# An RWKV scan in chunks: the state kept as one block-diagonal tile for two heads, and a chunk's products grouped by their shape on the array

## The reference, cut to what matters

```python
def step(state, inp):
    r_t, w_t, k_t, v_t, kk_t, b_t = inp
    sa = jnp.einsum('bhij,bhj->bhi', state, -kk_t)
    state = (state * w_t[:, :, None, :]
             + sa[..., None] * b_t[:, :, None, :]
             + v_t[..., None] * k_t[:, :, None, :])
    y_t = jnp.einsum('bhij,bhj->bhi', state, r_t)
    return state, y_t
```

## Time and profile before

| | us |
|---|---|
| median of 3 runs | 1783.13 |
| lowest and highest run | 1780.41, 1783.81 |
| span of the profiled execution | 1782.2 |
| TensorE busy in it (matmuls) | 1641.4 |
| VectorE, ScalarE, GpSimd busy | 882.9, 659.2, 122.8 |

### The profile page before, as it was taken

One profiled execution on the slowest core, in us unless ns is written; L12 is line 12 of the kernel. 1 busy time (PEld: TensorE's weight loads), 2 busy tenths in 40 slices (PEclk: granted clock), 3 DMA queues, 4 the chain that ended last, 5 costly groups with the idle time before them and its releaser, 6 DMA issues.

```text
span 1782.2 us, 36627 instructions
## 1 busy us (share of the span) xinstructions
PE 1641.4 (92%) x15044; PEld 1028.8 (58%) x15044; DVE 882.9 (50%) x1880; ACT 659.2 (37%) x1316; POOL 122.8 (7%) x311
## 2 busy tenths in 40 slices
PE   5999999999899989999999999999999988777798
PEld 2465565654654575868676767676754544333443
DVE  1371450732614466777777777878630542111163
ACT  2151431622412465565646565556510112111113
POOL 7000010000000000000000000000000012121100
PEclk9999999999999999999999999999999979999999
DMA  9230110301200321121202021111044579999831
GB/s 354 90 93 2 47 49 0 96 0 47 95 7 14 99 68 54 31 82 33 71 26 71 28 70 44 53 50 48 3 160 173 212 274 419 421 421 408 319 155 48
DMA packets 105463, 210.95 MB, mean 118 GB/s; under 512 B 10195, under 2 KB 78136, under 8 KB 92029
## 3 DMA queue, kind: packets, MB, share of 16 engines
q1 hardware_dynamic: 99256, 197.52, 30.6%
q0 software_dynamic: 4896, 8.40, 1.3%
q10 hardware_dynamic: 1188, 3.28, 0.5%
HBM read 203.80 MB, written 14.81 MB: 123 GB/s over the span
## 4 chain that ended last, share of the span: by engine, by line
PE 52%; DMA 10%; DVE 4%; ACT 2%; issue 2%; SPq 0%; DVEq 0%; ACTq 0%; POOL 0%; POOLq 0%
PE ps L1452 11%; DMA W<-in_moe_w_up_dram 7%; PE ps L2491 5%; PE ps L1463 5%; PE ps L1624 4%; PE ps L1593 4%; PE ps L3073 3%; PE ps L2887 3%; DMA W<-in_moe_w_gate_dram 3%; PE ps L506 2%; PE ps L1493 2%; PE ps L1474 1%; PE ps L1503 1%; PE ps L1515 1%; PE ps L1478 1%
## 5 line engine op out<-in xcount | busy, mean ns | idle before, releaser
L1452 PE MATMUL ps<-hT,W 128*128 128x512 f32 x512 | 231.8, 597 | 2.2 <-ACTq L95 2.2
L1452 PEld LDWEIGHTS ps<-hT,W 128*128 128x128 f32 x512 | 95.6, 191 | 99.9 <-issue 98.1
L594 PE MATMUL ps<-hT,W 128*128 128x512 f32 x288 | 141.0, 612 | 4.2 <-DVE spare L189 4.2
L1463 PE MATMUL ps<-W,hT 128*128 128x256 f32 x512 | 124.0, 388 | 0.0
L2035 DVE SCALAR_TENSOR_TENSOR arena<-ps,arena 128x510 f32<-128x510 f32 (+1 forms) x128 | 95.4, 745 | 12.3 <-ACT arena L1754 8.9
L1463 PEld LDWEIGHTS ps<-W,hT 128*128 128x128 f32 x512 | 93.1, 190 | 12.8
L2491 PE MATMUL ps<-W,yT 128*128 128x512 f32 x216 | 93.1, 592 | 0.9 <-ACT yT L1847 0.9
L1857 ACT ACTIVATE W<-ps 128x512 f32<-128x512 f32 x96 | 57.5, 599 | 70.9 <-PE ps L1593 30.7
L1624 PE MATMUL ps<-W 64*64 64x64 f32 x2304 | 77.2, 220 | 0.0
L594 PEld LDWEIGHTS ps<-hT,W 128*128 128x128 f32 x288 | 49.4, 190 | 45.9 <-issue 44.2
L2887 PE MATMUL ps<-W,yT 128*32 128x256 f32 x1024 | 59.6, 388 | 17.0 <-DMA W<-in_moe_w_gate_dram 10.7
(11 more groups left out here) (535 smaller groups left out, 2925.7 us busy)
## 6 DMA issues: line engine op xcount, KB each, us to landing
W<-in_w_in_dram SPq DMA_DIRECT2D x33, 512.0 KB, 6.6
W<-in_gdn_w_in_dram SPq DMA_DIRECT2D x16, 1024.0 KB, 7.6
arena<-in_moe_w_up_dram SPq DMA_DIRECT2D x16, 1024.0 KB, 18.4
arena<-in_moe_w_down_dram SPq DMA_DIRECT2D x16, 1024.0 KB, 17.0
W<-in_moe_w_up_dram SPq DMA_DIRECT2D x16, 1024.0 KB, 5.8
W<-in_moe_w_down_dram SPq DMA_DIRECT2D x16, 1024.0 KB, 18.3
W<-in_moe_w_gate_dram SPq DMA_DIRECT2D x16, 1024.0 KB, 17.4
arena<-in_moe_w_gate_dram SPq DMA_DIRECT2D x14, 1024.0 KB, 19.4
```

Of the source, the lines that this page charges most:

```text
L594: mm = pe.matmul(ps[:, 5 + i % 2, :], w[:, k, j, :], hT[:, k, :], start=(k == 0), stop=(k == ND - 1))
L1452: mm = pe.matmul(ps[:, 6 + k0 % 2, :], wg[:, k, j * P:(j + 1) * P], hT[:, k, :], start=(k == 0), stop=(k == ND - 1))
L1463: mm = pe.matmul(ps[:, 4 if t < 2 else 1, 256 * (t % 2):256 * (t % 2) + 256], hT[:, k, t * P:(t + 1) * P], wz[:, k, :], start=(k == 0), st ...
```

## The change

A tile `Sd` of 128x128 is added, `state_diagonal`. Head 0's state stands in its upper left quarter, head 1's in the lower right one, and the other two quarters are set to zero once, by GpSimd, before the loops.

- RU: for `c` above 0, one product of `AR` (all 128 partitions) by `Sd` gives both heads' state part in 128 columns of bank 0, and the two products of `Q` add to the two halves of it. In chunk 0, where the state is zero, only the two products of `Q` are issued.
- Y: its state part is one product, `Sd` by `AR`, issued right behind RU and ahead of slot 0; in chunk 0 it is left out. The other four products of Y add to it. They now stand right behind S1, ahead of slot 2.
- S1 and Y take the two heads in turn for each kind of product, where before they took all kinds for one head and then for the other. In the last chunk S1 is left out, since nothing reads it.
- ScalarE's copy of RU reads one bank.
- VectorE no longer clears `S0` and no longer waits for Y before the scaling. In chunk 0 it scales straight from PSUM. After the scaling it copies the two quarters into `Sd`, and the step that TensorE waits for is counted behind the second copy.

```diff
@@ setup @@
+    Sd = sb("state_diagonal", [P, P])
...
@@ tensor engine, chunk loop @@
-                pe.wait_ge(*rw_dve.at(f"S0 {c}", n))
+                if c:
+                    pe.wait_ge(*rw_dve.at(f"S0 {c}", n))
+                    pe.matmul(ps[:, 0, 0:P], AR[:, c, 0, :], Sd[:], start=True, stop=True)
                 for h in range(2):
                     r = slice(h * HD, h * HD + HD)
-                    pe.matmul(ps[:, 4 * h, 0:HD], AR[r, c, 0, :], S0[r, :], start=True, stop=False)
-                    mm = pe.matmul(ps[:, 4 * h, 0:HD], Q[:, h, c, 2, :], tok[:, c, 2, r], start=False, stop=True)
+                    mm = pe.matmul(ps[:, 0, r], Q[:, h, c, 2, :], tok[:, c, 2, r], start=(c == 0), stop=True, skip_group_check=bool(c))
                 mm.then_inc(*rw_pe.step(f"RU {c}"))
+                if c:
+                    pe.matmul(ps[:, 7, cs], Sd[:], AR[:, c, 1, :], start=True, stop=True)
...
+                if c < NT - 1:
+                    for h in range(2):
+                        r = HALF[h]
+                        pe.matmul(ps[r, 2, 0:HD], tok[:, c, 0, r], U[:, r], start=True, stop=False)
+                    for h in range(2):
+                        r = HALF[h]
+                        mm = pe.matmul(ps[r, 2, 0:HD], tok[:, c, 1, r], tok[:, c, 2, r], start=False, stop=True)
+                    mm.then_inc(*rw_pe.step(f"S1 {c}"))
                 for h in range(2):
-                    r = slice(h * HD, h * HD + HD)
-                    pe.matmul(ps[r, 2, 0:HD], tok[:, c, 0, r], U[:, r], start=True, stop=False)
-                    mm = pe.matmul(ps[r, 2, 0:HD], tok[:, c, 1, r], tok[:, c, 2, r], start=False, stop=True)
-                mm.then_inc(*rw_pe.step(f"S1 {c}"))
+                    r = HALF[h]
+                    pe.matmul(ps[r, 7, cs], U[:, r], Q[:, h, c, 1, :], start=(c == 0), stop=bool(c), skip_group_check=bool(c))
+                for h in range(2):
+                    r = HALF[h]
+                    mm = pe.matmul(ps[r, 7, cs], tok[:, c, 2, r], Q[:, h, c, 3, :], start=False, stop=True, skip_group_check=bool(c))
+                mm.then_inc(*rw_pe.step(f"Y {c}"))
                 fill(c, 2)
-                for h in range(2):
-                    r = slice(h * HD, h * HD + HD)
-                    pe.matmul(ps[r, 7, cs], U[:, r], Q[:, h, c, 1, :], start=True, stop=False)
-                    pe.matmul(ps[r, 7, cs], tok[:, c, 2, r], Q[:, h, c, 3, :], start=False, stop=False)
-                    mm = pe.matmul(ps[r, 7, cs], S0[r, :], AR[r, c, 1, :], start=False, stop=True)
-                mm.then_inc(*rw_pe.step(f"Y {c}"))
                 fill(c, 3)
@@ scalar engine @@
-                act.activation(RU.rearrange("p (h t) -> p h t", h=2), ps[:, 0:5:4, 0:HD], ACT.Copy).then_inc(*rw_act.step(f"RU {c}"))
+                act.activation(RU, ps[:, 0, 0:P], ACT.Copy).then_inc(*rw_act.step(f"RU {c}"))
@@ gpsimd, before the loops @@
+        pool.memset(Sd[:], 0.0).then_inc(*lo_pool.step())
@@ vector engine @@
-            link(dve.memset(S0, 0.0), "S0 0")
             for c in range(NT - 1):
                 dve.wait_ge(*rw_pe.at(f"S1 {c}", n))
-                link(dve.tensor_tensor(S1, ps[:, 2, 0:HD], S0, ALU.add))
-                dve.wait_ge(*rw_pe.at(f"Y {c}", n))
-                link(dve.tensor_scalar(S0, S1, fac[:, 1, c:c + 1], None, ALU.mult), f"S0 {c + 1}")
+                grown = ps[:, 2, 0:HD]
+                if c:
+                    link(dve.tensor_tensor(S1, grown, S0, ALU.add))
+                    grown = S1
+                link(dve.tensor_scalar(S0, grown, fac[:, 1, c:c + 1], None, ALU.mult))
+                for r in HALF:
+                    dve.tensor_copy(Sd[r, r], S0[r, :]).then_inc(*rw_dve.step(f"S0 {c + 1}"))
```

## The result

The changed kernel takes 1736.67 us (1734.89 to 1740.12) against 1781.77 us (1779.33 to 1783.81) for the kernel before, measured again beside it. The ratio is 0.9751, with a 95% interval of 0.9736 to 0.9766. That is 45.1 us less. Of the 7.2 us between 1743.9 and 1736.67, 1.3 are the starting point, which I had at 1783.1, and 5.9 are a larger saving. The profiled execution went from 1782.2 to 1733.1 us.

The account below looks back on a forecast made before the run. The prediction took TensorE's queue to bound the chunk loops. Savings of 28.9 us in pairs 0 to 2 and 10.3 in the last, together 39.2, took 1783.1 to 1743.9 us, with a range of 1739 to 1755.

Parts of the forecast that it names:

- 1743.9: Whole kernel: the forecast median in us, 1783.1 less a saving of 39.2; the band 1742 to 1748 had chance 0.71.
- the starting point: Whole kernel before the change: median taken as 1783.1 us, 0.9 above the profiled span of 1782.2.
- TensorE's queue is the bound in the loops: Chunk loops: in three of four pairs the loop takes what TensorE's queue takes, busy 46.90 of 46.90 us.
- RU and the state part at 0.11 a record: RU and Y's state part, chunks 1 to 3: 8 records of one shape, 0.90 us against RU's 1.36.
- S1 with Y at 0.90: S1 and Y, each chunk: 16 records of one shape take 0.90 us against 2.26, bounds 0.80 and 1.28.
- The serial bound of 1.28: S1 with Y: 1.28 us if records run one after the other; part of the dearer-records rival, chance 0.17.
- the heads in turn: S1 and Y: heads alternating between column halves make the halves overlap, so 0.90 us instead of 1.28.
- Slots 2 and 3 at 3.49: Fill slots 2 and 3, pairs 0 to 2: one run of 8 records, 3.49 us against 3.83, saving 0.34.
- Sums: Chunk loops: 9.62 us saved a pair in pairs 0 to 2, 28.9 for three, and 10.3 in the last.
- The wait for the copies costs nothing: Ahead of RU, chunks 1 to 3: VectorE's 1.6 us chain is covered by 4.0 us, 2.3 in the last pair.
- The failed step: Behind the loops: everything waits for TensorE's steps and moves forward, so the loops' 39.2 us is the whole saving.
- The range: Whole kernel: 1739 to 1755 us, from the larger gain with 2 us of scatter to dearer records nearly both at once.

Follow-up runs that it names:

- experiment 4: The changed kernel with S1 and Y ordered head by head again, everything else as changed: 1738.26 us, ratio 0.9771.
- experiment 6: The changed kernel with eight more linked multiplications by one on VectorE ahead of the two copies into the diagonal tile: 1737.41 us, ratio 0.9747.
- experiment 1: The changed kernel with 115 empty instructions on TensorE's queue at the start: 1749.89 us, ratio 0.9823.
- experiment 2: The kernel before with 141 empty instructions on TensorE's queue at the start: 1781.18 us, ratio 0.9997.
- experiment 7: The changed kernel with 60 empty instructions on TensorE's queue at the start, within its wait there: 1736.26 us, ratio 0.9747.
- experiment 5: Kernel before with only the diagonal tile; S1 and Y head by head, slot 2 between them, last chunk's S1 kept: 1742.63 us, ratio 0.9776.
- experiment 11: The changed kernel with the 2 MB reload of x issued later, behind U of the last pair's first chunk: 1736.56 us, ratio 0.9748.
- experiment 3: Kernel before with only S1, Y and the slots regrouped, heads in turn; 64-column state and RU as before: 1763.27 us, ratio 0.9889.
- experiment 9: Kernel before with S1, Y, the slots and also RU grouped by shape, without the diagonal tile: 1750.34 us, ratio 0.9818.
- experiment 10: The kernel before with the 2 MB reload of x issued later, behind U of the last pair's first chunk: 1782.10 us, ratio 1.0000.

## Why the prediction was right or wrong, point by point

- *TensorE's queue is the bound in the loops*: right. It was busy for 36.22 of 36.22 us after as well, and in the last pair for 21.88 of 22.76.
- *RU and the state part at 0.11 a record*: 0.90 forecast, 0.90 measured. Chunk 0's RU: 0.39 and 0.39 (148.61 to 149.00).
- *S1 with Y at 0.90*: measured 0.82, and Y alone in the last chunk 0.59 for 0.54. The serial bound of 1.28 does not hold here. The rule of the Trainium skill that a weight load overlaps a running matmul only when their row groups differ (TensorE: Matmul & The Clock Gate, What overlaps and what doesn't) would have given that bound, and the 0.82, all on the same rows, speaks against it. But the reason that I gave, the heads in turn, is worth only 0.05 a chunk by experiment 4.
- *Slots 2 and 3 at 3.49*: 3.54.
- *Sums*: 9.62 a pair forecast, 9.72 measured; last pair 10.3 and 10.39. The chunk period in the last pair was 5.35 for 5.5.
- *The wait for the copies costs nothing*: right. The chain took 1.2 us where I had 1.6, since linked steps follow each other after 0.03 and not 0.1 us, the two copies take 0.41 and not 0.5, and TensorE starts 0.05 behind them (experiment 6) and not 0.2. That TensorE had to wait for VectorE nowhere was true of the loops alone: in the delta net it waits 4.3 us for it at L1593.
- *The failed step* is in the total: "Everything behind the loops waits for TensorE's steps ... so I let it all move forward", with the saving set equal to that of the loops. I counted the instructions taken out of the program only by their own time, and not for moving what stands behind them. The stalls of the delta net went from 10.6 to 5.2 us, and between the marks the kernel gained 4.5; ahead of the last pair's loop it gained 4, by a shorter stall and, in this execution, a clock that did not fall. Experiments 1, 2 and 7 move the stalls by padding alone, record for record, and the first two cost 4.1 and gain 3.8 us in the delta net. The stalls were in the trace before (10.6 us of "issue"), and I did not read them because no edit touched them.
- *The range* was worked out from the prices of the loops alone and had 2 us of scatter as its only allowance below, so it ended at 1739. The starting point of 1783.1 alone would not have put the time outside: by the 1781.77 measured beside the changed kernel the forecast is 1742.6 and the lower end 1737.7, still above 1736.67, though by only 1 us.

The account of the profiled executions is 39.6 (loops) + 4 (ahead of the last loop) + 4.5 (delta net) + 1.9 (behind it, scatter) - 1.0 (start) = 49. The medians differ by 45.1, 4 less; single executions of one kernel lie up to 9 us apart. By medians the saving beyond the loops is 4.7 to 8.8 us in the six versions that have the delta net's stall at another place and pay for no padding (the changed kernel and experiments 4, 5, 6, 7 and 11), and -1.8 to +4.1 in experiments 3, 9 and 10, where the stall in the delta net kept its place. So that there is a surplus, and that it goes with the place, is shown. Its size is not: experiment 9 has 4.1 us of it with no stall moved, and the clock scatters too (between the marks it fell twice in the trace before, once in that of the changed kernel). The stalls go with packets of the program. Why they are 0.6 us long at one place and 1.0 to 1.9 at another, and why the other packets cause none, stays open.

The two parts compare as follows: grouping alone 32.5 us (experiment 9), the diagonal tile alone 41.0 (experiment 5), both 45.1; in the loops, by the profile, 28.4, 32.9 and 39.6. They overlap, because both remove changes of shape. No version tried was faster than the changed kernel beyond its interval.

## What to carry to other kernels

Where TensorE's queue is the bound and products are small, the order of their shapes can cost a good part of what the products cost: measure a block from its start to the start of the next, compare runs of one shape with mixed ones, and put equal shapes side by side before thinking of fewer products, above all where they use different halves of the array. When instructions go from or come into a long program, look at the "issue" waits of everything behind them as well, since the stalls there can move by several microseconds though no line of that code changed, and keep the range open for it on both sides.

## What was not expected of the hardware

- Products on the two row halves overlap: four records of 64*128 in 0.37 us (experiment 9), where two had taken 0.36 (before, with another shape between the halves). A change of shape cost about 0.14 us.
- Products on the two column halves overlap even when one head's four records come first in the program: 8 records in 0.59 us (experiment 4), against 0.11 a record on the whole array. The other head's first records begin ahead of this head's last ones.
- An empty instruction that raises a semaphore took 0.15 us on TensorE's queue (141 of them: 21.3 us; 115: 17.3).
- TensorE's stalls without a visible cause stand at fixed places of its program, move by one matmul record for two instructions, and end 1.24 to 1.61 us behind the end of a 16 KB packet of the instruction queue (118 stalls in 13 traces).
- Behind an idle time of TensorE of 1.6 to 4.0 us at this one place the granted clock fell to the 1.2 GHz level in 12 of 13 profiles. It stayed at 2.4 GHz in the changed kernel, with 1.59 us, and behind a second stall in experiment 5, with 1.68; with 1.61 us (experiment 4) it fell. So the length of the stall does not tell it.
